# First block's attention: values formed already turned, by products on TensorE's two column halves

## The reference, cut to what matters

```python
def attend(qblk):
    s = jnp.einsum('bqkgd,bskd->bkgqs', qblk, k, preferred_element_type=jnp.float32) * scale
    p = jax.nn.softmax(s, axis=-1).astype(v.dtype)
    return jnp.einsum('bkgqs,bskd->bqkgd', p, v)
...
ya = att @ w_branch[:ATT_Q_W]
yh = hy @ w_branch[ATT_Q_W:ATT_Q_W + HY_W]
yf = fn @ w_branch[ATT_Q_W + HY_W:]
m = jax.nn.sigmoid(ga) * ya + jax.nn.sigmoid(gh) * yh + jax.nn.sigmoid(gf) * yf
```

## Time and profile before

| what | us |
|---|---|
| three runs, median (lowest to highest) | 2299.32 (2298.85 to 2299.82) |
| the profiled execution | 2296.84 |
| its span | 2295.5 |
| TensorE busy | 1927.1 |
| VectorE busy | 982.9 |
| ScalarE busy | 668.9 |
| mean clock granted to TensorE | 0.936 of full |

### The profile page before, as it was taken

The page is one execution under the profiler, slowest core; times in us unless marked ns, Lnnn a source line. Parts: engine busy times, 40 slices in busy tenths (PEclk is TensorE's granted clock), DMA queues, the critical chain, the costliest instruction groups (busy, mean ns, idle before and its releaser), DMA issues.

```text
span 2295.5 us, 28914 instructions
## 1 busy us (share of the span) xinstructions
PE 1927.1 (84%) x12324; PEld 1348.0 (59%) x12324; DVE 982.9 (43%) x1219; ACT 668.9 (29%) x811; POOL 66.8 (3%) x144
## 2 busy tenths in 40 slices
PE   7899998556555566655589999999999999999998
PEld 4777962111111111111137998779998999778997
DVE  4745651000000000000006657875667666876656
ACT  4432420000000000000004444554445444455444
POOL 0000000000000000000001001010000000100000
PEclk9999999887878888787899999999999999999999
DMA  9156899999999999999997564245544555324552
GB/s 373 67 197 233 320 388 429 431 431 431 431 431 429 432 431 431 430 430 433 431 399 282 195 207 157 110 149 188 196 165 175 185 198 181 141 100 168 199 193 85
DMA packets 53489, 647.44 MB, mean 282 GB/s; under 512 B 5936, under 2 KB 6448, under 8 KB 10096
## 3 DMA queue, kind: packets, MB, share of 16 engines
q1 hardware_dynamic: 53360, 645.59, 70.5%
HBM read 644.52 MB, written 1.05 MB: 281 GB/s over the span
## 4 chain that ended last, share of the span: by engine, by line
PE 57%; DMA 32%; DVE 7%; ACT 2%; issue 1%; POOL 0%; SPq 0%; DVEq 0%; ACTq 0%; POOLq 0%
DMA wide_b<-in_experts 29%; PE PS L488 14%; PE PS L490 13%; PE PS L489 13%; PE PS L986 4%; PE PS L951 4%; DMA ring<-in_wgt 1%; DMA ahead<-in_wmod 1%; DVE low L1895 1%; PE PS L929 1%; DVE low L1409 1%; PE PS L641 1%; DVE PS L1920 1%; PE PS L1263 1%; DVE XR L1959 1%
## 5 line engine op out<-in xcount | busy, mean ns | idle before, releaser
L1895 DVE TENSOR_TENSOR low<-ring,WH 128x2048 fp32r<-128x2048 f32 (+1 forms) x163 | 372.1, 2283 | 182.5 <-ACT WH L2284 179.9
L488 PE MATMUL PS<-XH,WH 128*128 128x256 f32 x1408 | 396.9, 282 | 3.4 <-DVE XL L1927 3.3
L489 PE MATMUL PS<-XL,WH 128*128 128x256 f32 x1408 | 395.1, 281 | 0.0
L490 PE MATMUL PS<-XH,low 128*128 128x256 f32 x1408 | 393.1, 279 | 0.0
L2284 ACT ACTIVATE WH<-ring 128x2048 fp32r<-128x2048 f32 (+1 forms) x164 | 313.1, 1909 | 26.9 <-DMA ring<-in_fg 18.9
L488 PEld LDWEIGHTS PS<-XH,WH 128*128 128x128 f32 x1408 | 264.5, 188 | 7.0 <-issue 5.2
L490 PEld LDWEIGHTS PS<-XH,low 128*128 128x128 f32 x1408 | 267.5, 190 | 0.0
L489 PEld LDWEIGHTS PS<-XL,WH 128*128 128x128 f32 x1408 | 264.6, 188 | 1.4
L1877 DVE TENSOR_TENSOR T1S<-T1S,PS 128x512 f32<-128x512 f32 x16 | 11.0, 688 | 536.7 <-PE PS L951 536.7
L951 PE MATMUL PS<-ring,big 128*32 128x512 f32 x936 | 133.8, 721 | 57.9 <-DMA ring<-in_experts 57.9
L2558 ACT ACTIVATE T1S<-PS 128x512 f32<-128x512 f32 x16 | 9.6, 597 | 540.2 <-PE PS L951 540.2
(11 more groups left out here) (447 smaller groups left out, 2816.1 us busy)
## 6 DMA issues: line engine op xcount, KB each, us to landing
wide_b<-in_experts SPq DMA_DIRECT2D x30, 4096.0 KB, 23.7
wide_a<-in_experts SPq DMA_DIRECT2D x29, 4096.0 KB, 23.8
ring<-in_experts SPq DMA_DIRECT2D x28, 4096.0 KB, 24.0
ring<-in_fg SPq DMA_DIRECT2D x44, 1024.0 KB, 5.0
ring<-in_fu SPq DMA_DIRECT2D x44, 1024.0 KB, 5.0
ring<-in_fd SPq DMA_DIRECT2D x44, 1024.0 KB, 4.9
ring<-in_wmod SPq DMA_DIRECT2D x22, 1024.0 KB, 5.8
ring<-in_wgt SPq DMA_DIRECT2D x12, 1024.0 KB, 9.2
```

The source lines that it names most:

```text
L488: t.matmul(o, l[0], r[0], start=start, stop=False, skip_group_check=True)
L489: t.matmul(o, l[0], r[1], start=False, stop=False, skip_group_check=True)
L490: return t.matmul(o, l[1], r[0], start=False, stop=stop, skip_group_check=True)
L1895: own(v.tensor_tensor(low[:, w.slot.index, 0:size], w.flat, WH[:, w.slot.index, 0:size].bitcast(f32), ALU.subtract).then_inc(*c.wl.up()), ...
```

## The change

The exponentials become the moving operand and the values the stationary one. For two heads at once (`i` = 0, 1; one pair n in each odd round g = 2n + 3), a 128x64 piece of `VV` is held on column half i of the array and 128 columns of `PT[:, i]` move, over four pieces of keys. The result has channels on the partitions (two heads of 64) and queries on the columns, in bank 4 or 5, columns 0 to 127: it is turned already. The section 3 of even rounds forms no values any more, and `c.pv` rises by two at the end of each pair.

The denominators are per query, which is now along the columns. So VectorE forms their reciprocals for two heads (128x2) and multiplies them into the identity matrix, giving two diagonal 128x128 matrices (`scale`, 128x256 numbers). TensorE multiplies 128x64 ones with each of them, on column half i, which spreads 1/denominator over 64 partitions (bank 9-b, columns 128 to 255). ScalarE copies that to SBUF, and VectorE multiplies it with the values straight into `attT`. The division at the end, the eight transposes L797 and the four copies to `attT` are gone.

```diff
--- before.py
+++ after.py
@@ -233,6 +233,7 @@
         HP = XN[:, 0, 0:516].rearrange("p (a b) -> p a b", a=2)
         HS = XN[:, 1, :].rearrange("p (i a b) -> p i a b", i=2, a=2)
         attT = QT[:, 0:4, :]
+        scale = AT[:, :, :].rearrange("p m (a i c) -> p (m a) i c", a=2, i=2)
         hyT = QT[:, 4:6, :]
         fnT = QT[:, 6:8, :]
         z2 = T1[:, 0:512].rearrange("p (m c) -> p m c", m=2)
@@ -752,15 +753,26 @@
                     held[2 + b] = [(c.pca, (g - 1) // 2 + 1) if b else (c.pcv, (g - 1) // 2 + 1)]
                     step()
                 if g > 1:
-                    m, b = (g - 2) // 2 % 2, g % 2
-                    h = 2 * ((g - 2) // 4) + b
-                    take(2 + b)
-                    for i in range(4):
-                        x = t.matmul(PS[:, 4 + m, h * 64:h * 64 + 64], PT[:, b, i * 128:i * 128 + 128],
-                                     VV[:, i, b * 64:b * 64 + 64], start=i == 0, stop=i == 3)
-                    x.then_inc(*c.pv.up())
+                    if g % 2:
+                        n = (g - 3) // 2
+                        b = 4 + n % 2
+                        take(9 - b)
+                        P.wait_ge(c.at, n + 1)
+                        for i in range(2):
+                            x = t.matmul(PS[64 * i:64 * i + 64, 9 - b, 128:256], cd[:, 2, 0:64], scale[:, n % 4, i, :],
+                                         start=True, stop=True)
+                        x.then_inc(*c.atp.up())
+                        take(b)
+                        P.wait_ge(c.pcv, n + 1)
+                        P.wait_ge(c.pca, n + 1)
+                        for k in range(4):
+                            for i in range(2):
+                                x = t.matmul(PS[64 * i:64 * i + 64, b, 0:128], VV[:, k, i * 64:i * 64 + 64],
+                                             PT[:, i, k * 128:k * 128 + 128], start=k == 0, stop=k == 3,
+                                             skip_group_check=True)
+                        x.then_inc(*c.pv.up(2))
+                        held[b], held[9 - b] = [(c.attv, n + 1)], [(c.atta, n + 1)]
                     step()
-            held[4], held[5] = [(c.at, 1)], [(c.at, 2)]
 
 
             def spectrum(order):
@@ -789,16 +801,6 @@
                 held[2] = [(c.lz, order + 1)]
 
             spectrum(0)
-            for m in range(2):
-                take(2 + m)
-            for m in range(2):
-                P.wait_ge(c.at, m + 1)
-                for k in range(4):
-                    x = t.transpose(PS[:, 2 + k // 2, (k % 2) * 256 + m * 128:(k % 2) * 256 + m * 128 + 128],
-                                    AT[:, m, k * 128:k * 128 + 128], ident)
-                    if k % 2:
-                        x.then_inc(*c.atp.up())
-            held[2], held[3] = [(c.attv, 1)], [(c.atta, 1)]
             P.wait_ge(c.fx, 1)
             for i in range(2):
                 take(4 + i)
@@ -1646,17 +1648,23 @@
                         if g > 2:
                             V.wait_ge(c.pv, g - 2)
                         own(v.tensor_copy(PT[:, 0, :], PS[:, 2, :]).then_inc(*c.pcv.up()), c.pcv)
+                    elif g:
+                        n = (g - 2) // 2
+                        r = den[:, 0, n % 2, n // 2 * 2:n // 2 * 2 + 2]
+                        V.wait_ge(c.ex, g)
+                        own(v.reciprocal(r, r))
+                        if n > 3:
+                            V.wait_ge(c.pv, 2 * (n - 3))
+                        own(v.tensor_tensor(scale[:, n % 4], ident.unsqueeze(1).to_broadcast([128, 2, 128]),
+                                            r.unsqueeze(2).to_broadcast([128, 2, 128]), ALU.mult).then_inc(*c.at.up()), c.at)
                     step()
                 if g > 1:
-                    m = g - 16
-                    if m >= 0:
-                        V.wait_ge(c.ex, 14 + 2 * m)
-                        own(v.reciprocal(den[:, 0, m, :], den[:, 0, m, :]))
-                        V.wait_ge(c.pv, 14 + 2 * m)
-                        own(v.tensor_tensor(AT[:, m, :].rearrange("p (h d) -> p h d", h=8),
-                                            PS[:, 4 + m, :].rearrange("p (h d) -> p h d", h=8),
-                                            den[:, 0, m, :].unsqueeze(2).to_broadcast([128, 8, 64]),
-                                            ALU.mult).then_inc(*c.at.up()), c.at)
+                    if g > 3 and (g % 2 == 0 or g == 17):
+                        n = (g - 3) // 2
+                        V.wait_ge(c.atta, n + 1)
+                        V.wait_ge(c.pv, 2 * n + 2)
+                        own(v.tensor_tensor(attT[:, n // 2, n % 2 * 128:n % 2 * 128 + 128], PS[:, 4 + n % 2, 0:128],
+                                            scale[:, n % 4, 0, :], ALU.mult).then_inc(*c.attv.up()), c.attv)
                     step()
 
 
@@ -1689,13 +1697,6 @@
 
             V.wait_ge(c.u, 3)
             spectrum(0)
-            V.wait_ge(c.atp, 3)
-            for k in range(2):
-                i = v.tensor_copy(attT[:, k, :], PS[:, 2, k * 256:k * 256 + 256])
-                if k:
-                    own(i.then_inc(*c.attv.up()), c.attv)
-                else:
-                    own(i)
             V.wait_ge(c.ff, 1)
             own(v.tensor_copy(PB[:, 0, :], PS[:, 4, :]).then_inc(*c.ffv.up()), c.ffv)
             step()
@@ -2477,6 +2478,10 @@
                         own(copy(PT[:, 1, :], PS[:, 3, :]).then_inc(*c.pca.up()), c.pca)
                     step()
                 if g > 1:
+                    if g > 3 and (g % 2 == 0 or g == 17):
+                        n = (g - 3) // 2
+                        A.wait_ge(c.atp, n + 1)
+                        own(copy(scale[:, n % 4, 0, :], PS[:, 5 - n % 2, 128:256]).then_inc(*c.atta.up()), c.atta)
                     step()
 
 
@@ -2490,9 +2495,6 @@
                     own(a.activation(g, g, ACT.Sigmoid).then_inc(*c.sg.up()), c.sg)
                     signed += 1
 
-            A.wait_ge(c.atp, 4)
-            own(copy(attT[:, 2, :], PS[:, 3, 0:256]))
-            own(copy(attT[:, 3, :], PS[:, 3, 256:512]).then_inc(*c.atta.up()), c.atta)
             A.wait_ge(c.ff, 2)
             own(copy(PB[:, 1, :], PS[:, 5, :]).then_inc(*c.f1a.up()), c.f1a)
             step()
```

## The result

| | before | changed |
|---|---|---|
| median of 20 runs each, side by side (lowest to highest), us | 2298.75 (2294.24 to 2302.32) | 2301.47 (2296.58 to 2306.2) |
| ratio, changed to before (95% interval) | | 1.0013 (1.0007 to 1.0019) |
| the profiled execution, us | 2296.84 | 2306.2 |
| its span, us | 2295.5 | 2304.9 |
| mean clock granted to TensorE | 0.936 | 0.924 |

The change makes the kernel slower by 1.6 to 4.4 us, 3.0 in the middle.

A forecast was written before the change was run, and what follows sets the result against it. TensorE was taken as the bound in the attention, then DMA to 1220 us. Work -4.3, waits +3.2 and round 3 +2.1 gave +1.0 us, so 2300.3 us; range 2295.0 to 2304.8 (chance 0.82).

The forecast's parts named there:

- TensorE's own work: Attention: value products and transposes save 14.5 us, eight pairs at 1.27 us add 10.2, so work falls by 4.3 us.
- rivals 2 and 3: Pair steps: column halves run one after the other, 2308.9 us; or weight loads aren't hidden, 2304.8 us; chance 0.08 each.
- rival 3: Pair steps: weight loads not hidden between column halves, 4.5 us in all, giving 2304.8 us; chance 0.08.
- The side engines: Attention: new diagonals, products into `attT` and copies add 7.4 us on VectorE and 2.2 on ScalarE, covered by idle time.
- The waits in rounds 7, 11 and 15: TensorE idles 1.65 us before each bank 7 quarter, 4.9 us in all, replacing 1.7 us of idle time: net +3.2.
- Rival 1: VectorE's queue in the attention: the waits don't bite and the 4.3 us pass on whole, 2295.0 us; chance 0.12.
- no load becomes the last to arrive: Weight tile loads in the attention: issue moves by +0.5 to +1.3 us, the split still done before the pair ends.
- Round 3: Before the first filter spectrum TensorE loses 1.7 us, before the second 0.55; less 0.14 idle before, +2.1 us.
- The sum at the Fourier products: At L806, end of the attention: -4.3 + 3.2 + 2.1 = +1.0 us, starting at 198.0 instead of 196.97.
- I carry a shift at 197 us to the end one to one: From the attention's end to the kernel's end: the shift passes whole; at most 4.5 us of idle DMA time swallows it.
- the shift at L806 is not the shift at the end of the experts: Sign of a wrong prediction: the shift at the Fourier products differs from that at the experts' end (1219 us).

The follow-up runs named there:

- second profile: The changed kernel profiled and run again without an edit: 2301.93 us, ratio 1.0016 (1.0007 to 1.0024).
- second profile of before: The kernel before profiled and run again without an edit: 2298.57 us, ratio 0.9998 (0.9988 to 1.0008).
- the twelve profiles: One profile for each kernel or repeat of the study, both kernels taken twice; medians from 2296.58 to 2307.63 us.
- gate_out first: Changed kernel with `gate_out` ahead of VectorE's copy to `PT` in rounds 7, 11 and 15: 2298.21 us, ratio 1.0002 (0.9994 to 1.0010).
- pairs formed late: Kernel before with both old-form value products of a pair formed in the odd round, so `c.pv` rises late: 2307.63 us, ratio 1.0041.
- undivided one: Changed kernel with the division by the denominators left out, values copied undivided into `attT`: 2297.80 us, ratio 0.9999 (0.9988 to 1.0009).
- two filled ones: Identity products in TensorE's idle time: in the changed kernel, ratio 1.0009; in the changed kernel with `gate_out` first every odd round from 3, ratio 0.9988.

## Why the prediction was right or wrong

The forecast was 2300.3 us, +1.0; measured are 2301.47 and +3.0 (1.6 to 4.4). The time lies in the range, but the range is 10 us wide and the forecast shift of +1.0 lies outside of the measured interval. That the time came within 1.2 us is in part luck: the median of before, to which the shift was added, came out 0.6 us lower over 20 runs than over the three it was taken from. The steps up to 198 us held, the last one didn't.

- TensorE's own work. Forecast: 1.27 us for a pair with its spread products, 0.1 each way for the mode included. Measured: 133.49 to 134.53 from the first start to the last, and 1.24 us to the next product wherever that one doesn't wait. The steps are 0.11 us apart, both column halves at once, and loads don't show: rivals 2 and 3 are out. The rule of the Trainium skill behind rival 3 (TensorE: Matmul & The Clock Gate, Part 3: Packing small matmuls) doesn't hold for halves any more than for quarters: 16 loads on shared rows pass under 16 products.
- The side engines. 0.425 for the diagonals, 0.291 into `attT`, 0.278 for ScalarE's copy: forecast 0.42, 0.3, 0.27. All of it was covered.
- The waits in rounds 7, 11 and 15. Forecast 1.65 us, measured 1.62, three times in the second profile. Rival 1 is out: with the waits taken away by the order of the queue the stretch falls by 3.0 us, against 3.2 in the sum. The sentence that no load becomes the last to arrive failed in one of two profiles (10.10 us in round 15, 0.6 us more).
- Round 3. Forecast 1.7 and 0.55, measured 1.64 and 0.42 to 0.43.
- The sum at the Fourier products. Forecast 198.0, second profile 197.82, its stretch +0.99. Both terms were a little small and cancel: TensorE's busy time in the stretch falls from 103.6 to 98.9 us (-4.7, forecast -4.3), its idle time rises from 2.8 to 8.5 (+5.7, forecast +5.3).
- "I carry a shift at 197 us to the end one to one" is the step that failed, and it was wrong by its omission, as far as the runs tell, not by its rate. 3.0 and 4.2 us of the stretch gave 3.2 and 4.1 at the end. But the sign that the prediction had named for this step came: the shift at L806 is not the shift at the end of the experts. Counted from the first score product, the second profile of the changed kernel stands at +1.0 us at the Fourier products (+1.1 against the second profile of before), at +1.9 (+2.4) at the router's gather and at +6.5 (+6.8) at the last products of the experts; from there to the end it takes 0.5 us less than the first profile of before and 1.5 more than the second. These profiles lie apart by more than the medians do (before below its median, changed above), so the stages show where the shift grows, not how much of the +3.0 each holds.
- The first cost that was left out is the load of the ninth gate tile: TensorE is idle for 2.34 us there, instead of 1.12 or 0.65 in the two profiles of before, so +1.2 to +1.7. No row of before showed it, since there the packet starts as the load lands.
- The second lies at the end of the experts and is the largest one behind the attention in both profiles. TensorE waits for the last wide tile of an expert for longer, and the clock falls for 6.8 us. Before, then the second profile of the changed kernel:

```profile
1206.92 1.92 PE L986 MATMUL PS<-wide_b,PBT 128*32 128x512 f32 x16 [2.20 <-DMA wide_b<-in_experts]
```

```profile
1210.68 3.64 PE L988 MATMUL PS<-wide_b,PBT 128*32 128x512 f32 x16 [3.55 <-DMA wide_b<-in_experts]
```

In the twelve profiles a fall stands at this wait in the four where it lasted 3.4 to 3.7 us (both of the changed kernel, gate_out first, pairs formed late), and in none of the eight with 0.85 to 2.8. From there to the experts' last products it is 12.15 us in the eight and 13.5 to 15.0 in the four. From the four turning products ahead of this wait (L977, L979) to the end of the span both profiles of the changed kernel are 3.4 to 3.7 us longer than the first of before, and 4.9 to 5.2 longer than the second. Why the tile comes late, and whether the change causes it, wasn't tried.

- Falls of the clock in the attention are the third, and only a chance. They come at the idle times that the change makes: behind round 15 in one of two profiles of the changed kernel, twice in the one with late pairs, twice in the undivided one, and in none of the two of before nor in the two filled ones. Three more (232 to 237 us) stand at the wait for the ninth gate tile in other kernels, where its load took 11.6 to 12.0 us; in the changed kernel the same load had none. Of the +3.0, the stretch accounts for 1.0 and the ninth load for about 1.2; the remaining 0.8 is a remainder, not a measurement, and how the last two causes share it is open.

## What to carry to other kernels

When two releases of a semaphore become one later one, go to the first instruction that waits for it and walk down its queue: here the copy could wait, and what stood behind it could not, so swapping the two was worth about as much (4.2 us of the stretch) as the new form of the products (4.7 us of TensorE's busy time). Put whatever empties the bank that the busy engine takes next ahead of any wait on that same engine. A shift of 1 us is also within what other events do downstream (a packet of instructions that falls into a critical load, a fall of the clock behind idle time), so a forecast of that size needs room on the slow side for each new idle time.

## What the runs showed of the hardware

- Float32 products of 128 columns on two column halves start in pairs 0.11 us apart, with their weight loads hidden, as fast as single products of 128 columns on the whole array (eight of L797 in 0.87 us).
- In 5 of 19 cases in the attention, over the twelve profiles, an idle time of 1.6 to 2.2 us on TensorE came with a fall of the granted clock from 1.00 to 0.51 or 0.52 for 3.4, 6.8 or 10.2 us, which began late in the idle time or within 1.6 us behind it. Products of 256 columns then start 0.21 instead of 0.12 us apart.
- Ninety-six more instructions on TensorE, placed some 190 us earlier and out of the way, made a 1 MB load 1.0 to 1.5 us longer (11.63 against 10.63 and 10.17), through the place of one 16 KB packet of the instruction queue.
